# Query-state products between the large products of an input unit; means and pooling behind the next unit

## What is computed

```python
def retention(q, k, v, S0):            # 8 heads of 64; prompt: 2 chunks of 128 tokens; sample: 1 token each
    def step(S, qkv):
        qc, kc, vc = qkv
        sc = jnp.einsum('bnhd,bmhd->bhnm', qc, kc) * dmask[None]
        inner = jnp.einsum('bhnm,bmhe->bnhe', sc, vc)
        cross = jnp.einsum('bnhd,bhde->bnhe', qc, S) * xi[None, :, :, None]
        S = S * g_c[None, :, None, None] + jnp.einsum('bmhd,bmhe->bhde', kc * zeta[None, :, :, None], vc)
        return S, inner + cross

def mixer(hn, buf, S, pos0, w_in, w_pool, pool_scale, w_o):
    z = jnp.einsum('bld,de->ble', hn, w_in)          # u (512), q, k, v, g (512 each)
    ...
    o, S_new = retention(q, k, v, S)
    mu = jnp.mean(o, axis=-1, keepdims=True)
    var = jnp.mean(jnp.square(o - mu), axis=-1, keepdims=True)
    o = ((o - mu) * lax.rsqrt(var + NORM_EPS)).reshape(B, L, RET_WIDTH)
    o = o * jax.nn.silu(g.astype(jnp.float32))
    pool_out, buf_new = pool_mixer(u, buf, pos0, w_pool, pool_scale)
    mix = jnp.concatenate([pool_out, o], axis=-1).astype(hn.dtype)
    return jnp.einsum('ble,ed->bld', mix, w_o), buf_new, S_new.astype(S.dtype)
```

## Time and profile before

| | us |
|---|---|
| median of 3 runs | 900.12 |
| lowest, highest | 899.53, 902.18 |
| the profiled execution, its own time | 900.8 |
| span of its instructions | 899.0 |
| TensorE busy | 873.0 (97%) |
| VectorE busy | 697.2 (78%) |
| ScalarE busy | 540.7 (60%) |
| GpSimd busy | 176.4 (20%) |

### The profile page before, as it was taken

One profiled execution on the slowest core, in us unless ns is written; L12 is line 12 of the kernel. 1 busy time (PEld: TensorE's weight loads), 2 busy tenths in 40 slices (PEclk: granted clock), 3 DMA queues, 4 the chain that ended last, 5 costly groups with the idle time before them and its releaser, 6 DMA issues. The chain is left out here.

```text
span 899.0 us, 14456 instructions
## 1 busy us (share of the span) xinstructions
PE 873.0 (97%) x5919; PEld 759.1 (84%) x5919; DVE 697.2 (78%) x793; ACT 540.7 (60%) x659; POOL 176.4 (20%) x190
## 2 busy tenths in 40 slices
PE   6999999999999999999999999999999999999995
PEld 6999999999999999999877677777777777777794
DVE  5796676555555588786679988899898989898976
ACT  5446555443435455345467877787787877876752
POOL 5456321100110013564211410002000010010012
PEclk9999999999999999998999999999999999999998
DMA  9992565545553644944418999999999999999801
GB/s 340 361 331 78 189 206 207 194 153 200 190 182 130 222 159 178 294 152 154 144 65 297 420 350 367 395 367 393 359 392 371 387 383 371 402 359 389 340 2 48
DMA packets 50419, 236.51 MB, mean 263 GB/s; under 512 B 4810, under 2 KB 8170, under 8 KB 42624
## 3 DMA queue, kind: packets, MB, share of 16 engines
q1 hardware_dynamic: 44672, 215.51, 64.4%
q0 software_dynamic: 4960, 18.96, 7.2%
q10 hardware_dynamic: 720, 1.10, 0.3%
HBM read 226.38 MB, written 8.55 MB: 261 GB/s over the span
## 5 line engine op out<-in xcount | busy, mean ns | idle before, releaser
L1573 DVE TENSOR_TENSOR wlo<-raw,whi 128x1408 fp32r<-128x1408 f32 (+2 forms) x292 | 468.5, 1638 | 95.7 <-ACT whi L1283 95.5
L1283 ACT ACTIVATE whi<-raw 128x1408 fp32r<-128x1408 f32 (+2 forms) x292 | 392.8, 1377 | 140.8 <-PE bank L727 78.2
L725 PE MATMUL bank<-xh,whi 128*128 128x264 f32 x672 | 194.4, 289 | 9.0 <-DVE xl L1584 8.3
L726 PE MATMUL bank<-xl,whi 128*128 128x264 f32 x672 | 192.1, 286 | 0.0
L727 PE MATMUL bank<-xh,wlo 128*128 128x264 f32 x672 | 191.8, 285 | 0.0
L1090 PE MATMUL bank<-whi,xeh 128*96 128x512 f32 (+1 forms) x384 | 143.8, 374 | 1.4 <-DVE wlo L1573 0.8
L1091 PE MATMUL bank<-wlo,xeh 128*96 128x512 f32 (+1 forms) x384 | 143.5, 374 | 0.0
L1092 PE MATMUL bank<-whi,xel 128*96 128x512 f32 (+1 forms) x384 | 143.2, 373 | 0.0
L725 PEld LDWEIGHTS bank<-xh,whi 128*128 128x128 f32 x672 | 128.2, 191 | 10.7 <-DVE wlo L1966 8.2
L726 PEld LDWEIGHTS bank<-xl,whi 128*128 128x128 f32 x672 | 128.3, 191 | 0.2
L727 PEld LDWEIGHTS bank<-xh,wlo 128*128 128x128 f32 x672 | 127.6, 190 | 0.0
(11 more groups left out here) (264 smaller groups left out, 1206.2 us busy)
## 6 DMA issues: line engine op xcount, KB each, us to landing
raw<-in_moe_w_gate SPq DMA_DIRECT2D x32, 1408.0 KB, 8.8
raw<-in_moe_w_up SPq DMA_DIRECT2D x32, 1408.0 KB, 9.3
raw<-in_moe_w_down SPq DMA_DIRECT2D x40, 1024.0 KB, 8.2
raw<-in_w_in SPq DMA_DIRECT2D x17, 1024.0 KB, 6.1
raw<-in_ffn_w_down SPq DMA_DIRECT2D x16, 704.0 KB, 4.2
raw<-in_ffn_w_gate SPq DMA_DIRECT2D x10, 1024.0 KB, 4.8
raw<-in_ffn_w_up SPq DMA_DIRECT2D x10, 1024.0 KB, 5.0
raw<-in_w_o SPq DMA_DIRECT2D x8, 1024.0 KB, 10.5
```

What stands on the lines that cost most here:

```text
L725: pe.matmul(out, w_hi, x_hi, start=start, stop=False)
L726: pe.matmul(out, w_hi, x_lo, start=False, stop=False)
L1283: act.activation(unit_hi(u), unit_raw(u), ACT.Copy).then_inc(hi_ready, 1)
L1573: dve.tensor_tensor(unit_lo(u), unit_raw(u), unit_hi(u).bitcast(F32), ALU.subtract).then_inc(lo_ready, 1)
```

## The change

The query-state products leave the side steps' place. In `chunk`, behind the three large products of each k step of unit nine, two of them are issued (`state_products`), 16 times two for both chunks; `unit_pair` first waits for what they read. `qS` moves to the front of `AFTER[8]`, which sets bank numbers and VectorE's order. Means and pooling now stand behind the second chunk of unit ten on TensorE, and VectorE's and ScalarE's orders follow (z chunk and silu of the last chunk ahead of them).

```diff
@@ -310,7 +310,7 @@
 AFTER = [["norm1"], [], [], [], [], [],
          ["vs", "vt0", "vt1"],
          ["sc00", "sc01", "kt0", "kt1", "win", "o0", "sc10", "sc11"],
-         ["S", "tail", "qS", "qk", "o1"],
+         ["qS", "S", "tail", "qk", "o1"],
          [f"mu{c}" for c in range(RC)] + ["wp0", "wp1", "wp2", "wp3"],
          ["va"] + [f"rb{c}" for c in range(RC)]]
 ROPE_AFTER = {4: 0, 5: 1}
@@ -731,7 +731,7 @@
                 for _ in range(count):
                     pe.matmul(bank[3][:, 0:T], ident, const[:, 0:T], start=True, stop=True)
 
-            def chunk(at, n, u, k, w, m, xhi, xlo, row_ready=None):
+            def chunk(at, n, u, k, w, m, xhi, xlo, row_ready=None, beside=None):
 
 
                 if at >= 4:
@@ -745,16 +745,21 @@
                         pe.wait_ge(ready, before + (kc + 1))
                     mm = weights_first(out, H[:, kc, m * P:(m + 1) * P], L[:, kc, m * P:(m + 1) * P],
                                        xhi[:, kc, :], xlo[:, kc, :], kc == 0, kc == k - 1)
+                    if beside is not None:
+                        layer, first = beside
+                        state_products(layer, first + 2 * kc)
                 return mm
 
-            def unit_pair(u, n, xhi, xlo, row_ready=None, between=None):
+            def unit_pair(u, n, xhi, xlo, row_ready=None, beside=None):
 
                 pe.wait_ge(lo_ready, u + 1)
-                chunk(n, n, u, DC, 256, 0, xhi, xlo, row_ready).then_inc(acc_full, 1)
-                if between is not None:
-                    for name in AFTER[9]:
-                        side_step(between, name)
-                chunk(n + 1, n + 1, u, DC, 256, 1, xhi, xlo).then_inc(unit_used, 1)
+                if beside is not None:
+                    pe.wait_ge(side_free, SIDE[beside, "qS"] - 3)
+                    pe.wait_ge(s_decayed, RC * (beside + 1))
+                    pe.wait_ge(qm_ready, 2 * (beside + 1))
+                chunk(n, n, u, DC, 256, 0, xhi, xlo, row_ready, None if beside is None else (beside, 0)).then_inc(acc_full, 1)
+                chunk(n + 1, n + 1, u, DC, 256, 1, xhi, xlo, None,
+                      None if beside is None else (beside, 2 * DC)).then_inc(unit_used, 1)
 
             def first_pair(u):
 
@@ -841,15 +846,14 @@
                     mm = pe.matmul(bank[4 + i % 4][0:NE, 0:T], wr[:, c, :], hg[:, c, :], start=(c == 0), stop=(c == DC - 1))
                 return mm
 
-            def state_products(l, b):
-
-                pe.wait_ge(s_decayed, RC * (l + 1))
-                pe.wait_ge(qm_ready, 2 * (l + 1))
-                for s in range(NS):
-                    for c in range(RC):
-                        a = 2 * (s * RC + c)
-                        mm = pe.matmul(b[0:HD, a:a + 2], S[:, s, c, :], qm[:, s, c, :], start=True, stop=True)
-                return mm
+            def state_products(l, first):
+
+                b = bank[side_bank(l, "qS")]
+                for n in (first, first + 1):
+                    own, c = divmod(n, RC)
+                    mm = pe.matmul(b[0:HD, 2 * n:2 * n + 2], S[:, own, c, :], qm[:, own, c, :], start=True, stop=True)
+                    if n == NS * RC - 1:
+                        mm.then_inc(side_full, 1)
 
             def side_step(l, name):
                 i = SIDE[l, name]
@@ -936,8 +940,6 @@
                                 mm = pe.matmul(b[own, c * CH:(c + 1) * CH], sbd[:, c, own], qxi[:, c, :], start=False, stop=True)
                                 if c == RC - 1 and a == 0:
                                     mm.then_inc(side_full, 1)
-                elif name == "qS":
-                    mm = state_products(l, b)
                 elif name == "qk":
                     pe.wait_ge(qkp_ready, l + 1)
                     mm = pe.matmul(b[:, 0:RC * NS], C("hmean"), qkp[:, :, :].rearrange("p c s -> p (c s)"), start=True, stop=True)
@@ -1206,11 +1208,11 @@
                     four_chunks(U_MIX[1], A_MIX[1], PARTS_AT[3], (1, "norm1"), 2)
                 for j in range(10):
                     if j > 1:
-                        unit_pair(U_MIX[l] + j, A_MIX[l] + 2 * j, xh, xl, between=l if j == 9 else None)
+                        unit_pair(U_MIX[l] + j, A_MIX[l] + 2 * j, xh, xl, beside=l if j == 8 else None)
                     elif l == 0:
                         first_pair(j)
-                    for name in AFTER[j] if j < 9 else ():
-                        if name not in ("norm1", "sc01", "sc11"):
+                    for name in AFTER[j]:
+                        if name not in ("norm1", "sc01", "sc11", "qS"):
                             side_step(l, name)
 
                 side_step(l, "va")
@@ -1479,6 +1481,7 @@
                             ins = act.activation(vb[half][:, b, c, :], vb[half][:, b, c, :], ACT.Copy, scale=qk[:, 1, c, at:at + 1])
                     ins.then_inc(kv_ready, 1)
                 silu_g_part(l, 2)
+                silu_g_part(l, 3)
                 for c in range(RC):
                     act.wait_ge(side_free, SIDE[l, f"mu{c}"] + 1)
                     act.activation(osq[:, c, :], oc[:, c, :], ACT.Square).then_inc(osq_ready, 1)
@@ -1487,7 +1490,6 @@
                     act.wait_ge(side_full, FULL[l, f"wp{g}"])
                     act.activation(mh[:, g, :], bank[side_bank(l, f"wp{g}")][:, 0:T], ACT.Copy,
                                    scale=pscale[:, l, g:g + 1]).then_inc(mix_hi, 1)
-                silu_g_part(l, 3)
                 act.activation(warm[:, :], C("eps", 1), ACT.Sqrt)
                 act.wait_ge(side_full, FULL[l, "va"])
                 act.activation(rvar[:, :], bank[side_bank(l, "va")][:, 0:T], ACT.Sqrt, bias=C("eps")).then_inc(stdv_ready, 1)
@@ -1979,8 +1981,7 @@
                     if j == 0:
                         side_step(l, "norm1")
                     z_chunk(l, 2 * j)
-                    if j < 9:
-                        z_chunk(l, 2 * j + 1)
+                    z_chunk(l, 2 * j + 1)
                     for name in AFTER[j]:
                         if name == "norm1":
                             continue
@@ -1988,8 +1989,6 @@
                         if name == "tail":
                             for g in range(PC):
                                 pool_diff(l, g)
-                    if j == 9:
-                        z_chunk(l, 2 * j + 1)
                     if j in ROPE_AFTER:
                         dve.wait_ge(const_in, 64)
                         rope(l, ROPE_AFTER[j])
```

## The result

| | before | after |
|---|---|---|
| median of the runs | 901.70 (10 runs) | 913.06 (10 runs) |
| lowest, highest | 897.38, 904.71 | 905.20, 922.25 |
| the profiled execution, its own time | 900.8 | 915.99 |
| span of its instructions | 899.0 | 914.2 |

What follows compares the result with a forecast made beforehand. TensorE, busy 873.0 of 899.0 us, was taken as the bound. Groups +15.8, block -8.0, clock -4.5, wait +0.4 and moved means 0 gave +3.7, so 903.8, range 899 to 913.

Steps and rivals of the forecast that it cites:

- the case that I called likeliest: Whole program: switches in unit nine are paid and the clock stays full, +3.7, so 903.8; chance 0.60.
- the rival with the clock for one layer: Unit nine: the clock falls to half, giving 913 for one layer or 922 for both; chance 0.16.
- Groups of unit nine: Unit nine: three large and two tiny products take 0.87 instead of 0.36; +15.8 for both layers.
- Block gone, o1 at full clock: Behind unit nine: the query-state block's removal saves 8.0 in both layers; o1 at full clock saves 1.6 and 1.7.
- Wait for sbd: In front of o1: a new wait for VectorE's state copy, 0.2 a layer, 0.5 at worst; +0.4 in all.
- Clock: the step that failed: Behind the removed block: full clock for o1, and for line 943 and unit ten of layer 1; -4.5.
- Moved means and pooling: 0: Behind unit ten: the moved work's followers still fit, so 0, with up to 1 us a layer for the range.
- The chances: Whole program against before: slower by over 0.3% 0.72, within 0.16, faster 0.12.
- Hidden products: Unit nine: weight loads hide even across shape changes, a group costs only 0.24 more, 895.7; chance 0.12.
- The cheaper switch: Unit nine: a group takes between 0.60 and 0.80, say 0.79, giving 901.4; chance 0.12.

Runs made afterwards that it cites:

- half the switches: The changed kernel with four tiny products behind every second k step instead of two behind each; 901.40, ratio 1.0004.
- only the interleaving and the adds held: The changed kernel with means, pooling and last silu back between unit ten's chunks, and GpSimd's sample-state adds waiting for o1's copy; 909.29, ratio 1.0112.
- the longer streams: The changed kernel with each query-state product streaming all query columns from its own on, 64 falling to 2; 907.89, ratio 1.0086.
- alternating halves: The kernel before, with query-state products of odd pairs of heads sent to the upper 64 partitions of the bank; 895.13, ratio 0.9950.
- differences behind: The changed kernel with means, pooling and last silu back between unit ten's chunks, and VectorE's pooling differences behind o1's copy; 932.25, ratio 1.0334.

## Why the prediction was right, and where it was not

The direction and the size of the switches were right; the case that I called likeliest was not the usual one. The forecast was 3.7 above before; the median is 11.4 above, the ratio gives 9. 913.06 lies on the upper bound of the range, where I had put the rival with the clock for one layer. That it lies there is luck: in the profile the clock fell in both layers, for which I had 922, but each time only half-way through the unit, and in three of ten runs, by their mean clocks, not at all.

*Groups of unit nine.* Forecast 0.87, measured 0.885. The kernel with half the switches prices one pair of them at 0.28, and the one without them has a group of 0.58.

*Block gone, o1 at full clock.* Best read in the two stretches above with only the interleaving and the adds held, since there the clock never fell: 18.31 against 15.34, +2.97, and 18.32 against 15.80, +2.52. By my terms it would be 7.9 - 3.93 - 1.6 + 0.2 = 2.57 and 7.9 - 4.11 - 1.7 - 0.2 + 0.2 = 2.09. The rest, 0.4 a layer, is the next term (0.3) and the 0.015 of each group (0.2), less 0.1 elsewhere. The span of that execution is 902.4, 3.4 above before, and the sum was 3.7; this nearness proves little, since the two layers give 5.5 - 0.95 = 4.5 and the idle entries in front of the pooling 0.95 more, and unit nine of layer 0 began 1.55 earlier than in before (65.67, 67.22) for reasons that aren't the change's. The changed kernel's own three runs at 0.995 to 0.997 lie 1.4 to 5.1 above the 903.8 forecast; none of them was profiled. Of that distance 0.8 is placed, and 1.6 is that before itself has a median of 901.70 over ten runs, not 900.12.

*Wait for sbd.* Taken as 0.2; it is 0.50 a layer at full clock, the worst end, and nothing where the clock is down.

*Clock: the step that failed.* "With the long run of query-state products gone, I expect the full clock in what follows", and 61.90 to 65.40 as the nearest row. That stretch of transposes said nothing for 14 us of alternating products. The mixture has 0.36 of large products in each 0.885 and otherwise two-column streams and switches. I read it now as the work that brought the clock down in before, diluted; the longer streams and the kernel with half the switches, which both kept the clock, fit that. It brought the clock down in the profile in both layers and, by their mean clocks (at most 0.989), probably in seven of ten runs. The rival had the mechanism and the cold group (forecast 1.45, measured 1.48), with too many cold groups: against 18.31 at full clock the layers lost 5.1 and 6.5, not 9.2 each, because the clock fell half-way through the unit. These 11.6 are most of the 15.2 between the spans. By these runs the chance of 0.16 should have been the largest one. The Trainium skill, TensorE: Matmul & The Clock Gate, section Part 1: The HAM clock gate, ties the lower clock to an idle TensorE; here TensorE shows no idle entry for 8 us ahead of each fall, and longer streams at the same number of products kept the clock, so the trace doesn't agree.

*Moved means and pooling: 0.* Alone it is worth nothing, and the uncovered wait is 0.17. But "nothing" held only for before: with the interleaving the same move spares 4 to 5 us. I had asked what the move uncovers and not what the missing block uncovers in front of the means: VectorE's pooling differences and GpSimd's adds, which the 3.9 of the block used to cover.

*The chances.* Two sums are off by 0.01: 0.60 - 0.05 + 0.16 is 0.71, and 0.12 + 0.05 is 0.17.

*The rivals.* Hidden products would need a group of 0.60, and that appears only with equal shapes. The cheaper switch is excluded by 0.885.

## What to carry over

Put tiny products between large ones in the shape of the large ones: here two products with 64-column weights between 128-column ones cost 0.28 for the switch there and back, more than their own four passes (0.24), while joining the two to one of 128 columns made the same idea a gain of 0.4%. Before a block is spread out, ask also what its time covered on the other engines, and whether the mixture that it makes keeps the clock. A block of small products may be cheaper to shorten (alternating halves, 3.8 to 2.0) than to hide.

## What the runs showed of the hardware

- The clock went to its lower level while TensorE was never idle: in unit nine of the changed kernel (75.0, 409.7), with 0.36 in 0.885 spent on 264-column products. The same number of products with streams of 64 falling to 2 columns kept 1.00, and so did the same products with half the switches (mean clock 0.994 to 0.997 in all twelve runs). It isn't fixed by the program: three runs of the changed kernel stayed at 0.995 to 0.997, and the version with the adds held kept 1.00 in unit nine in its profile.
- TensorE also lost the clock after idle of 3.2 (granted 0.67 in 89.00 to 98.00, differences behind): one stall of VectorE is paid twice. After idle of 1.31 in front of the pooling, in the version with alternating halves, line 954 took 2.05 for its eight passes, the time at full clock.
- Passes with 64-column weights, one after another, cost 0.06 when all results go to the same 64 partitions, whether they stream two columns or 64 falling to 2, and 0.031 when they alternate between the two halves of the partitions.
- VectorE and GpSimd exclude each other in some operations: a sum of 128x32 with both operands in SBUF took 2.19 instead of 0.19 and ended with GpSimd's add, one of 128x16 took 2.36 instead of 0.17, and a subtraction of 128x2048 3.97 instead of 2.28, while the copy from a bank just ahead of it (0.69, begun with GpSimd's add, alternating halves) was not held up. The Trainium skill, SBUF — State Buffer, section SBUF: two separate sides, has this as an exclusive lock on a shared pair of ports, held for the whole instruction; the traces agree, with 2.19 in place of 0.19.
